# Turning the attention heads' weights with VectorE blocks and a trip through HBM in place of TensorE

## The reference

```python
def stick_breaking_attention(h, w_in, q_gain, k_gain, w_out):
    ...
        z = jnp.einsum('bhqd,bhkd->bhqk', qb, k)
        strict = key_pos[None, :] < q_pos[:, None]
        log_1m = jnp.where(strict, jax.nn.log_sigmoid(-z), 0.0)
        rest = lax.cumsum(log_1m, axis=3, reverse=True) - log_1m
        a = jnp.where(strict, jnp.exp(jax.nn.log_sigmoid(z) + rest), 0.0)
        return jnp.einsum('bhqk,bhkd->bhqd', a, v)
    ...
    return o @ w_out
```

## Time and profile before

| what | value |
|---|---|
| median of the runs | 1209.72 us (1209.63 to 1209.78, 3 runs) |
| span of the profiled execution | 1207.7 us |
| the profiled execution's own time | not given beside its span; the runs' median is 2.0 us above the span |
| busy: TensorE, VectorE, ScalarE, GpSimd | 1202.5, 851.9, 582.1, 59.5 us |
| DMA | 229.58 MB, 190 GB/s on average |
| granted TensorE clock | full in all slices |

### The profile page before, as it was taken

The page is one execution under the profiler, slowest core; times in us unless marked ns, Lnnn a source line. Parts: engine busy times, 40 slices in busy tenths (PEclk is TensorE's granted clock), DMA queues, the critical chain, the costliest instruction groups (busy, mean ns, idle before and its releaser), DMA issues.

```text
span 1207.7 us, 14964 instructions
## 1 busy us (share of the span) xinstructions
PE 1202.5 (100%) x5420; PEld 997.4 (83%) x5420; DVE 851.9 (71%) x1104; ACT 582.1 (48%) x719; POOL 59.5 (5%) x101
## 2 busy tenths in 40 slices
PE   9999999999999999999999999999999999999998
PEld 7888888888888888888888888888888888888887
DVE  5897979889689676676587577677666666655554
ACT  6556475565655544443444444444444444444442
POOL 0302011011000200000000000000000000001000
PEclk9999999999999999999999999999999999999999
DMA  8665565655555766666666676666565656565663
GB/s 271 210 189 164 158 201 161 205 165 168 183 168 175 224 193 177 205 191 186 199 193 187 192 207 185 183 207 193 185 203 185 205 181 205 181 205 192 206 212 105
DMA packets 119850, 229.58 MB, mean 190 GB/s; under 512 B 7235, under 2 KB 8821, under 8 KB 119797
## 3 DMA queue, kind: packets, MB, share of 16 engines
q1 hardware_dynamic: 119764, 228.90, 61.7%
q10 hardware_dynamic: 32, 0.01, 0.0%
HBM read 226.78 MB, written 2.10 MB: 190 GB/s over the span
## 4 chain that ended last, share of the span: by engine, by line
PE 89%; DVE 5%; issue 0%; ACT 0%; DVEq 0%
PE acc L1109 87%; DVE w_lo L722 2%; DVE side L940 2%; PE T L1156 1%; DVE squares L787 1%; PE R L1174 0%; PE T L1184 0%; DVE xT_lo L951 0%; PE Z L1156 0%; PE acc L1319 0%; PE acc L1327 0%; ACT w_hi L458 0%; PE T L1166 0%; PE Z L1166 0%; PE T L1142 0%
## 5 line engine op out<-in xcount | busy, mean ns | idle before, releaser
L458 ACT ACTIVATE w_hi<-raw 128x1024 fp32r<-128x1024 f32 x425 | 448.6, 1059 | 540.2 <-PE acc L1109 535.2
L722 DVE TENSOR_TENSOR w_lo<-raw,w_hi 128x1024 fp32r<-128x1024 f32 x425 | 517.7, 1224 | 262.2 <-ACT w_hi L458 259.1
L1109 PE MATMUL acc<-w_hi,xT_hi 128*128 128x512 f32 x1200 | 469.8, 392 | 0.2 <-DVE w_lo L722 0.2
L1109 PE MATMUL acc<-w_hi,xT_lo 128*128 128x512 f32 x1200 | 467.1, 389 | 0.0
L1109 PE MATMUL acc<-w_lo,xT_hi 128*128 128x512 f32 x1200 | 467.0, 389 | 0.0
L1109 PEld LDWEIGHTS acc<-w_hi,xT_hi 128*128 128x128 f32 x1200 | 225.3, 188 | 48.2 <-issue 1.2
L1109 PEld LDWEIGHTS acc<-w_hi,xT_lo 128*128 128x128 f32 x1200 | 225.2, 188 | 47.1
L1109 PEld LDWEIGHTS acc<-w_lo,xT_hi 128*128 128x128 f32 x1200 | 225.4, 188 | 46.1
L1109 PE MATMUL acc<-w_hi,hT_hi 128*128 128x512 f32 x352 | 136.9, 389 | 0.0
L1109 PE MATMUL acc<-w_lo,hT_hi 128*128 128x512 f32 x352 | 136.9, 389 | 0.0
L1109 PE MATMUL acc<-w_hi,hT_lo 128*128 128x512 f32 x352 | 136.9, 389 | 0.0
(11 more groups left out here) (160 smaller groups left out, 630.8 us busy)
## 6 DMA issues: line engine op xcount, KB each, us to landing
raw<-in_sb_w_in SPq DMA_DIRECT2D x93, 512.0 KB, 4.0
raw<-in_ffn_w_gate SPq DMA_DIRECT2D x88, 512.0 KB, 3.7
raw<-in_ffn_w_up SPq DMA_DIRECT2D x88, 512.0 KB, 4.3
raw<-in_ffn_w_down SPq DMA_DIRECT2D x88, 512.0 KB, 4.3
raw<-in_sb_w_out SPq DMA_DIRECT2D x32, 512.0 KB, 3.8
raw<-in_ple_w_gate SPq DMA_DIRECT2D x32, 512.0 KB, 4.6
x<-in_x SPq DMA_DIRECT2D x8, 256.0 KB, 6.4
raw<-in_ple_w_proj SPq DMA_DIRECT2D x4, 512.0 KB, 6.5
```

Of the source, the lines that this page charges most:

```text
L458: act.activation(w_parts[0][:, slot(u), 0:n, :], raw[:, slot(u), 0:n, :], ACT.Copy).then_inc(hi_ready, 1)
L722: dve.tensor_tensor(w_parts[1][:, slot(u), 0:n, :], raw[:, slot(u), 0:n, :], w_parts[0][:, slot(u), 0:n, :].bitcast(F32), ALU.subtract).th ...
L1109: last = pe.matmul(acc[pair][tb][:, :], parts[a][:, c, tb * P:(tb + 1) * P], w_parts[w][:, slot(u), i, :], start=(start and i == 0 and n = ...
```

## The change

TensorE's turns go. VectorE turns each 32x32 block of the masked weights (`block_weights`, from `weight` to `w_blocks`), each within its place in the 4x4 grid: turned, but not moved across the diagonal. SyncE stores the tile to a scratch in HBM, 1536 B for each partition, and loads it back with four DMAs, one for each block row, each piece 384 B, so that the blocks land in their turned places (`move_weights`). ScalarE and VectorE make the high and low parts from that SBUF tile `w_side` and not from PSUM tile R.

The steps move too: VectorE's blocks at s + 6, SyncE's store behind its load of unit s + 10 and the four loads behind that of unit s + 11, ScalarE's copies and VectorE's low part at s + 9, TensorE's weighing ahead of unit s + 8, the output's storing at s + 11. Heads start at 0, 3, 6, 9 as before, in the last group at 0, 2, 3, 5. SyncE's two loops over groups and tiles are written out.

The diff, cut to its core; in the places left out `attend` gets `A_HEADS` or `B_HEADS` in place of `A_EVERY` or `B_EVERY`:

```diff
-    A_EVERY, B_EVERY = 3, 2
-    W_TURN, W_AT, V_AT = 3, 6, 3
+    A_HEADS, B_HEADS = (0, 3, 6, 9), (0, 2, 3, 5)
+    W_BLOCKS, W_MOVE, W_SPLIT, W_AT, V_AT = 5, 9, 8, 7, 3
     A_FROM, B_FROM = 1, 1
...
             weight = [at_row(f"weight{i}", [P, 3 * P]) for i in range(HG)]
+            w_blocks = [at_row(f"w_blocks{i}", [P, QN, 3, Q]) for i in range(2)]
+            w_side = [at_row(f"w_side{i}", [P, QN, 3, Q]) for i in range(2)]
+            w_scratch = [nc.dram_tensor(f"w_scratch{i}", [P, QN, 3 * Q], F32, kind="Internal").ap() for i in range(2)]
             p_sb = at_row("p_sb", [P, TB, KP * P])
...
         behind_ready = sem("behind_ready")
-        weight_turned = sem("weight_turned")
+        weight_blocks = sem("weight_blocks")
+        weight_stored = [sem(f"weight_stored{i}") for i in range(2)]
+        weight_moved = [sem(f"weight_moved{i}") for i in range(2)]
         exponent_ready = sem("exponent_ready")
...
+            def move_weights(h, i, part):
+
+                scratch = w_scratch[i % 2]
+                if part == 0:
+                    sp.wait_ge(weight_blocks, h + 1)
+                    if h >= 2:
+                        sp.wait_ge(weight_moved[i % 2], 16 * QN * (h // 2))
+                    sp.dma_start(scratch[:, :, :], w_blocks[i % 2][:, :, :, :].rearrange("p b k i -> p b (k i)")
+                                 ).then_inc(weight_stored[i % 2], 16)
+                else:
+                    sp.wait_ge(weight_stored[i % 2], 16 * (h // 2 + 1))
+                    if h >= 2:
+                        sp.wait_ge(weight_lo_ready, h - 1)
+                    for b in range(QN):
+                        sp.dma_start(w_side[i % 2][b * Q:(b + 1) * Q, :, :, :].rearrange("j a k i -> j a (k i)"),
+                                     scratch[:, b, :].rearrange("(a j) n -> j a n", j=Q)).then_inc(weight_moved[i % 2], 16)
+
+            def attend(u, g, heads):
+
+                for h in range(HG):
+                    for part in range(2):
+                        if u == heads[h] + W_MOVE + part:
+                            move_weights(g * HG + h, h, part)
+
             def group(g, skip=0):
                 for part in range(skip, 3):
-                    columns = w_in[:, part * D:(part + 1) * D][:, bass.ts(g, NT)]
                     for u in range(DU):
-                        load(A0 + g * AU + part * DU + u, part * DU + u, D_UNITS[u], columns)
+                        load(A0 + g * AU + part * DU + u, part * DU + u, D_UNITS[u],
+                             w_in[:, part * D + g * NT:part * D + (g + 1) * NT])
+                        if g > 0:
+                            attend(part * DU + u - A_FROM, g - 1, A_HEADS)
...
             group(0, skip=1)
-            with nc.Fori(1, GROUPS, engines=[mybir.EngineType.SP], hint_back_edge=True) as g:
+            for g in range(1, GROUPS):
                 group(g)
                 load(B0 + u, u, blocks, w_o[:, t * NT:(t + 1) * NT])
-            with nc.Fori(0, XN - 2, engines=[mybir.EngineType.SP], hint_back_edge=True) as n:
+                attend(u - B_FROM, GROUPS - 1, B_HEADS)
+            for n in range(XN - 2):
                 for u in range(DU):
-                    load(B2 + n * DU + u, u, D_UNITS[u], w_o[:, 2 * NT:][:, bass.ts(n, NT)])
+                    load(B2 + n * DU + u, u, D_UNITS[u], w_o[:, (2 + n) * NT:(3 + n) * NT])
+                    attend(BH + n * DU + u - B_FROM, GROUPS - 1, B_HEADS)
             with nc.Fori(0, FN, engines=[mybir.EngineType.SP], hint_back_edge=True) as j:
...
-                act.wait_ge(weight_turned, h + 1)
-                act.activation(wT1[i % 2][:, :], R[:, 2 * P:3 * P], ACT.Copy)
-                act.activation(wT0[i % 2][0][:, :], R[:, 0:2 * P], ACT.Copy).then_inc(weight_hi_ready, 1)
+                act.wait_ge(weight_moved[i % 2], 16 * QN * (h // 2 + 1))
+                act.activation(wT1[i % 2][:, :].rearrange("p (a i) -> p a i", i=Q), w_side[i % 2][:, :, 2, :], ACT.Copy)
+                act.activation(wT0[i % 2][0][:, :].rearrange("p (k a i) -> p k a i", a=QN, i=Q),
+                               w_side[i % 2][:, :, 0:2, :].rearrange("p a k i -> p k a i"), ACT.Copy).then_inc(weight_hi_ready, 1)
-            def attend(u, g, every):
+            def attend(u, g, heads):
                 for h in range(HG):
-                    if u == every * h + W_AT + 3:
+                    if u == heads[h] + W_AT + 3:
                         keep_o(g * HG + h)
-                    if u == every * h + W_TURN + 3:
+                    if u == heads[h] + W_SPLIT:
                         weights_hi(g * HG + h, h)
-                    if u == every * h + 4:
+                    if u == heads[h] + 4:
                         weights_of(g * HG + h, h)
-                    if u == every * h + 3:
+                    if u == heads[h] + 3:
                         softplus_of(g * HG + h, h)
...
+            def block_weights(h, i):
+
+                dve.wait_ge(weight_kept, h + 1)
+                if h >= 2:
+                    dve.wait_ge(weight_stored[i % 2], 16 * (h // 2))
+                dve.transpose(w_blocks[i % 2][:, :, :, :].rearrange("p b k i -> p k b i"),
+                              weight[i][:, :].rearrange("p (k b j) -> p k b j", b=QN, j=Q)).then_inc(weight_blocks, 1)
+
             def weights_lo(h, i):
                 dve.wait_ge(weight_hi_ready, h + 1)
-                parts = wT0[i % 2]
-                dve.tensor_tensor(parts[1][:, :], R[:, 0:2 * P], parts[0][:, :].bitcast(F32),
+                parts = [w[:, :].rearrange("p (k a i) -> p k a i", a=QN, i=Q) for w in wT0[i % 2]]
+                dve.tensor_tensor(parts[1], w_side[i % 2][:, :, 0:2, :].rearrange("p a k i -> p k a i"), parts[0].bitcast(F32),
                                   ALU.subtract).then_inc(weight_lo_ready, 1)
...
-            def attend(u, g, every):
+            def attend(u, g, heads):
                 for h in range(HG):
-                    if u == every * h + W_AT + 3:
+                    if u == heads[h] + W_AT + 3:
                         keep_o(g * HG + h)
-                    if u == every * h + W_TURN + 4:
+                    if u == heads[h] + W_SPLIT:
                         weights_lo(g * HG + h, h)
-                    if u == every * h + 3:
+                    if u == heads[h] + W_BLOCKS:
+                        block_weights(g * HG + h, h)
+                    if u == heads[h] + 3:
                         log_terms(g * HG + h, h)
...
-            def turn_weights(h, i):
-
-                pe.wait_ge(weight_kept, h + 1)
-                pe.wait_ge(weight_lo_ready, h)
-                for b in range(3):
-                    last = pe.transpose(R[:, b * P:(b + 1) * P], weight[i][:, b * P:(b + 1) * P], ident[:, :])
-                last.then_inc(weight_turned, 1)
-
             def weigh(h, i, g):
...
-            def attend(u, g, every):
+            def attend(u, g, heads):
                 for h in range(HG):
-                    if u == every * h:
+                    if u == heads[h]:
                         scores(g * HG + h, h, g)
                 for h in range(HG):
-                    if u == every * h + W_AT:
+                    if u == heads[h] + W_AT:
                         weigh(g * HG + h, h, g)
-                    if u == every * h + W_TURN:
-                        turn_weights(g * HG + h, h)
```

More of the change, by code:

```diff
@@ L602, in group @@
                             keep_v(g - 1, U0 - 1)
-                        attend(u - A_FROM, g - 1, A_EVERY)
+                        attend(u - A_FROM, g - 1, A_HEADS)
                     for part in range(2):
@@ L622, in _ @@
                     keep_v(GROUPS - 1, B0 - 1)
-                attend(u - B_FROM, GROUPS - 1, B_EVERY)
+                attend(u - B_FROM, GROUPS - 1, B_HEADS)
             for u in range(2 * DU):
@@ L627, in _ @@
                 if u == 0:
-                    attend(BH - B_FROM, GROUPS - 1, B_EVERY)
+                    attend(BH - B_FROM, GROUPS - 1, B_HEADS)
                 for t in range(LAST):
```

## The result

| kernel | median | runs | against before |
|---|---|---|---|
| before | 1209.63 us | 1209.33 to 1209.78 (5) | |
| changed | 1220.01 us | 1217.15 to 1220.76 (5) | 1.008 [1.0069, 1.0091] |

A forecast was written before the change was run, and what follows sets the result against it. TensorE, busy for practically the whole span, was taken as the bound. Turns removed -5.3, group ends +1.3, last group +0.7 gave -3.3 us: 1206.4 us; forecast's own range 1204.4 to 1207.3, 8-in-10 range 1204.3 to 1210.8, bounds 1204.4 to 1215.5.

The forecast's parts named there:

- The gain on TensorE: Three turns for each of 16 heads leave TensorE's chain, 0.33 us a head: 5.3 us, the whole possible gain.
- The block turn: On VectorE, a 128x384 block transpose per head takes 0.65 us, 10.4 us in all, mostly where VectorE waits anyway.
- The order on ScalarE: In unit 13 head 3's softplus starts earlier, at about 109.0, so VectorE's log terms start at 110.63 instead of 111.53.
- No cost from traffic and from SyncE being held: 6.3 MB more DMA traffic is no bound; weight loads held behind SyncE's waits have 4.2 us of cover.
- The place: In unit 18 ScalarE waits for head 3's loads before the two squares, making VectorE's sum of squares 0.8 us late.
- the cost of the round trip at the group ends: Head 3's trip through HBM makes TensorE lose 0.4 us at each of three group ends, 1.3 us.
- Heads 0 to 2 make the same trip ... and are free.: Their 7.2 us trips cost nothing, with VectorE further ahead and no squares behind them.
- The landings of head 3: DMA landings taken as 3.3 us for the store and 2.5 for the last small load; bounds 2.2 and 4.0.
- The slack of 0.36 us: At a group's end, VectorE's low parts for next unit 0 are done at 148.86; TensorE wants them at 149.22.
- In the last group: TensorE waits 0.7 us for the low part of head 2's weights; bounds 0 and 3.6 us.
- The weights of head 3: TensorE wants them for weighing at 128.8 and has them at 126.8, 2 us early.
- the same wait, slower: From 1.3 us more on head 3's round trip, waits exceed 5.3 + 2.4 us; 1213.2 at 1.5 more; chance 0.09.

The follow-up runs named there:

- late_split: The changed kernel with ScalarE's copies, VectorE's low part and the weighing one unit later for heads 0 to 11: 1210.4 us, ratio 1.0007.

## Why the prediction was wrong

- **The gain on TensorE** (5.3 us) was right: 5.1 measured without the turns.
- **The block turn** was right: 0.572 us against 0.65, and 9.2 us of it hidden on VectorE. The order on ScalarE was read rightly as well: with no wait for the pieces the log terms of head 3 start 2.85 us after its scores, against a forecast of 2.87.
- **No cost from traffic and from SyncE being held**: right, 1204.61 with everything but the wait.
- **The place** was right: ScalarE's wait in front of the two squares in unit 18, then VectorE's chain up to the next group's unit 0. It was only one of the places.
- **The step that failed is the cost of the round trip at the group ends**: 1.3 us in the sum, 8.3 measured. Three terms of it were off:
  - *"Heads 0 to 2 make the same trip ... and are free."* They were not. In the first group ScalarE's wait for head 1 delayed head 3's log terms and so its blocks by 1.4 us, in the other two the wait for head 2 delayed the blocks by 1.0. Together 3.4 us. I had left out what stands behind these copies in ScalarE's and VectorE's programs.
  - *The landings of head 3.* I took 3.3 us for the store and 2.5 for the last small load, between rows that gave 2.2 on an idle queue and 4.0 behind weights. In the first group they took 4.1 and 3.5 us (from about 124.7 to 128.2), 1.7 more; in the other two 3.1 and 3.2, then 3.6 and 2.7, 0.4 to 0.5 more. Together about 2.6 us. The same delay made the earlier heads late: head 2's store took 5.6 us in the second group (issued at 182.54).
  - *The slack of 0.36 us.* I had added eight units of 2.744 us to the time at which the chain begins, 127.27. The trace of before has TensorE at unit 0 at 148.91, and not at 149.22. Three times 0.36 is 1.1 us, and with the 1.3 forecast the terms come to 8.4. In the first group the sum of squares was 3.85 us late where I had 0.8, and 3.8 of it came out on TensorE.
- **In the last group** 0.7 us became 4.4, and there the trip was as forecast: counted from the group's first score product (294.95 before, 299.31 after), head 2's low part was done at 326.5, where I had 326.6. That is luck in part, since the first store was issued 0.9 us early and took 4.0 us instead of 3.3. What failed is a wait that I had left out: weighing head 2 waits for head 1's output to be stored, and ScalarE, stopped for head 2's pieces, stores it late (2.2 of the 2.4 us). And I had no term for the clock, 1.8 us.
- **The weights of head 3** were not 2 us early for TensorE but 1.27 us late in the first group. This lies within the group's loss.

My bounds, with 4.0 us for every landing, gave 1215.5, and even these were passed: they had the earlier heads free, the slack, and neither the wait for tile O nor the clock. The range was cut at 1210.8 because I gave the late trip 0.33 in all. The slope that I had worked out, 4.5 us for each us of trip, should have widened it: the forecast stood on two numbers for which the trace had only bounds, 1.8 us apart. And the rival "the same wait, slower" was the case, with a chance of 0.09.

What stays open: why the changed kernel's untraced executions take up to 3.6 us more than the traced one. The mean granted clock on record is 0.998 for the two fastest (1217.15 and 1218.05 us) and 0.997 for the three slower ones. That fits a second TensorE wait long enough to lower the clock, but no trace shows it.

## What to carry to other kernels

A short DMA on the path of a result can take the landing of whatever is moved ahead of it. In a stream of large loads, issue both legs of such a trip ahead of the large load of the step and let that load spend its cover; here moving the store alone won half, moving the loads alone lost, and a queue of its own lost. A wait in an engine's program also delays what stands behind it, so follow every trip through both of its engines, and not only the one whose place is known to be tight: here two trips called free cost 3.4 us. When a forecast hangs on one latency that the trace bounds only from both sides, multiply the distance between the bounds by the number of places that wait for it before choosing the range. And a step "one unit later" has a price where the engine behind it has no pause: 0.42 us of VectorE moved into such a stretch cost 0.34 us a group.

## What was not expected of the hardware

- The same store of 192 KB landed in a median of 2.1 or 2.5 us with no weight load of its step ahead of it, 4.1 with one (4.8 in the kernel with the later copies), 4.4 on GpSimd's queue beside them, and 5.1 behind a pile of them.
- After a stop of 2.4 us TensorE's granted clock was 0.50 for some 3 us, which cost 1.8 us on top of the stop. It stayed at 1.00 in the first group, with stops of 0.6 and 1.3 us. After the stop of 4.47 us in `late_split` it was 0.50 as well.
- A block turn of 128x384 on VectorE took 572 ns, where 32x256 took 436.
